# Column and row groups in the q, k, v projection, and the gate logarithms and transposes inside its block

## What is computed

```python
c_qkv, c_beta, c_a = split(hc @ w_in[:, :COL_Z], (COL_BETA, COL_A))     # context tokens
x_qkv, x_beta, x_a, ... = split(hx @ w_in, ...)                         # latent tokens
# gdn_scan, for both
qkv = silu(centred_depthwise_conv(p_qkv, conv_w))        # 5 taps
q, k, v = heads(split(qkv, 3))
q = l2_normalize(q) * HEAD_DIM ** -0.5                   # t * rsqrt(sum(t * t) + EPS)
k = l2_normalize(k)
beta = sigmoid(p_beta)                                   # 2 directions x 8 heads
g = -exp(a_log) * softplus(p_a + dt_bias)
# gated_delta_chunked
G = cumsum(g)                                            # inside a chunk
decay = exp(where(incl, G[..., :, None] - G[..., None, :], -inf))
low = where(strict, (k * beta) @ k.T * decay, 0)
T = inverse(eye + low)                                   # then the scan over the chunks
```

## Time and profile before

| | |
|---|---|
| median of 3 runs | 1741.42 us (1741.04 to 1742.06) |
| profiled execution, first to last instruction | 1744.5 us |
| PE busy | 1535.1 us (88%) |
| DVE, ACT, POOL busy | 811.9, 372.7, 190.5 us |
| mean granted clock of PE | 0.926 of 2.4 GHz |

### The profile page before, as it was taken

The page is one execution under the profiler, slowest core; times in us unless marked ns, Lnnn a source line. Parts: engine busy times, 40 slices in busy tenths (PEclk is TensorE's granted clock), DMA queues, the critical chain, the costliest instruction groups (busy, mean ns, idle before and its releaser), DMA issues. The chain is left out here.

```text
span 1744.5 us, 19526 instructions
## 1 busy us (share of the span) xinstructions
PE 1535.1 (88%) x7573; PEld 898.2 (51%) x7573; DVE 811.9 (47%) x1508; ACT 372.7 (21%) x704; POOL 190.5 (11%) x280
## 2 busy tenths in 40 slices
PE   4999968778999998775889869998989899999977
PEld 2877757478744444342334334443444456656663
DVE  2344548545446567722112123546655225575453
ACT  3122236111111100110001020100540234542230
POOL 0000015700000000011000000000440001213330
PEclk9899979777899999787899989999999899999988
DMA  9331002230497687689999985244220221121120
GB/s 350 106 91 54 0 1 49 82 92 11 129 321 271 232 306 258 276 322 408 410 365 366 390 318 176 97 157 142 64 73 12 85 97 49 49 97 49 50 73 25
DMA packets 132299, 283.62 MB, mean 163 GB/s; under 512 B 28744, under 2 KB 39272, under 8 KB 126955
## 3 DMA queue, kind: packets, MB, share of 16 engines
q1 hardware_dynamic: 128608, 266.65, 42.8%
q0 software_dynamic: 3600, 15.73, 2.2%
HBM read 312.77 MB, written 4.19 MB: 182 GB/s over the span
## 5 line engine op out<-in xcount | busy, mean ns | idle before, releaser
L2717 PE MATMUL ps<-hT,ring 128*128 128x512 f32 x256 | 113.4, 600 | 3.1 <-PEq L2624 2.7
L1402 PE MATMUL ps<-ring,hT 128*128 128x512 f32 x256 | 111.8, 593 | 1.9 <-PEq L184 1.8
L333 DVE SCALAR_TENSOR_TENSOR ada_acc<-ring,cact,ada_acc 128x512 f32<-128x512 f32 x154 | 104.1, 745 | 0.5
L638 PE MATMUL ps<-hT,ring 128*128 128x256 f32 x384 | 90.8, 392 | 5.3 <-PEq L184 5.3
L2352 PE MATMUL ps<-hT,ring 128*128 128x512 f32 x208 | 90.4, 592 | 0.0
L638 PEld LDWEIGHTS ps<-hT,ring 128*128 128x128 f32 x384 | 74.6, 197 | 19.5 <-issue 8.0
L2717 PEld LDWEIGHTS ps<-hT,ring 128*128 128x128 f32 x256 | 48.5, 193 | 61.9 <-issue 61.9
L1402 PEld LDWEIGHTS ps<-ring,hT 128*128 128x128 f32 x256 | 48.0, 190 | 60.3 <-issue 60.0
L1935 PE MATMUL ps<-ring,hT 128*32 128x512 f32 x384 | 54.3, 717 | 25.7 <-DMA ring<-in_expert_w 25.7
L729 DVE SCALAR_TENSOR_TENSOR conv<-xpad,taps,conv 128x512 f32<-128x512 f32 (+1 forms) x96 | 63.6, 663 | 3.4
L2352 PEld LDWEIGHTS ps<-hT,ring 128*128 128x128 f32 x208 | 39.5, 190 | 48.5 <-issue 48.3
(11 more groups left out here) (527 smaller groups left out, 2699.8 us busy)
## 6 DMA issues: line engine op xcount, KB each, us to landing
ring<-in_expert_w SPq DMA_DIRECT2D x24, 2048.0 KB, 15.2
far<-in_expert_w SPq DMA_DIRECT2D x24, 2048.0 KB, 18.3
ring<-in_w_in SPq DMA_DIRECT2D x16, 2048.0 KB, 10.7
ring<-in_ada_w SPq DMA_DIRECT2D x12, 2048.0 KB, 10.4
ring<-in_w_ada SPq DMA_DIRECT2D x12, 2048.0 KB, 9.0
ring<-in_w_in_c SPq DMA_DIRECT2D x10, 2048.0 KB, 7.9
ring<-in_expert_w POOLq DMA_DIRECT2D x32, 512.0 KB
far<-in_expert_w POOLq DMA_DIRECT2D x32, 512.0 KB
```

What stands on the lines that cost most here:

```text
L333: ins = dve.scalar_tensor_tensor(out=part, in0=slot[:, kt], scalar=c[:, kt:kt + 1], in1=part, op0=ALU.mult, op1=ALU.add)
L638: ins = pe.matmul(ps[:, j % BANKS, s * L:(s + 1) * L], slot[:, kt, (j % 4) * P:(j % 4 + 1) * P], (hTc, hTx)[s][:, kt], start=(kt == 0), st ...
L1402: ins = pe.matmul(ps[:, 2 + i % BANKS], hTx[:, kt, t * P:(t + 1) * P], stream.slot(n)[:, kt], start=(kt == 0), stop=(kt == KT - 1))
L2717: ins = pe.matmul(bank, slot[:, kt, j % 4 * P:(j % 4 + 1) * P], hT[:, kt], **edge)
```

## The change

- Beta and gate products: `wba` is stationary (32 columns) and 128 tokens are streamed; the four token tiles go to four quarters of the PSUM partitions. The result has the tokens in the free dimension, so DVE copies it and PE transposes it back before tile 4 (`turn_ba`); DVE splits it (`split_ba`).
- Sums of squares: four calls `sum_squares(b)`, each for four heads with 32 stationary columns into four quarters of bank 7. The squares get eight buffers, which lie in `ktok`.
- Spreads: four calls `spread_norm(b)`, each for four heads from four quarters of the rows into banks 4 to 7.
- The gates' logarithms on ACT move before tiles 9 and 16 (`gates_of_ba`, `logs_of_gates`), their parts on DVE to tiles 12, 15 and 18, the gates' sums on PE before tile 14 (`sum_gates`).
- The transposes follow tile 23 in the same block, k first. ACT copies out the first twelve; of the last four, which wait for silu of the last tile, ACT and DVE copy two each.
- The blocks of the transposes and of the gates' sums are gone. POOL's clears move into the preparation, ahead of the masks of g = 2 and g = 4, and SP waits for them before it loads the first solution.

```diff
...
+N_SQ = 2 * QUADS
+sq = ktok[:, :, :].rearrange("p t d -> p (t d)").rearrange("p (b t) -> p b t", b=N_SQ)
+quad = lambda g: slice(g * WIN, (g + 1) * WIN)
 ssem = stage_sems(scope, "qkv_")
 loaded, proj, padded, conved, silued = ssem("loaded"), ssem("proj"), ssem("padded"), ssem("conved"), ssem("silued")
 pad_zero, taps_t, taps_done = ssem("pad_zero"), ssem("taps_t"), ssem("taps_done")
+GATES_AT, SUM_AT, LOGS_AT = 9, 14, 16
+K_TURNS, V_TURNS = 4 * TT, 2 * TT
+N_TURNS = K_TURNS + 2 * V_TURNS
+def turn_of(i):
+    if i < K_TURNS:
+        return kT, ktok, i // 2, i % 2
+    return vT, vtok, (i - K_TURNS) % V_TURNS, (i - K_TURNS) // V_TURNS
+def move(eng, copy, i):
+    _, dst, t, half = turn_of(i)
+    eng.wait_ge(turned, i + 1)
+    return copy(dst[:, t, half * 512:half * 512 + 512], ps[:, 4 + i % 4])
...
-def sum_squares(j):
+def sum_squares(b):
+    if b == 0:
...
+    pe.wait_ge(squared, QUADS * (b + 1))
+    row = pick_row[:, WIN - 1 - b:2 * WIN - 1 - b]
+    ranges = [(L, 2 * L)] if b < 2 else [(0, L), (L, 2 * L)] if b == 2 else [(0, 2 * L)]
+    for a, e in ranges:
+        for g in range(QUADS):
+            ins = pe.matmul(ps[quad(g), 7, a:e], row, sq[:, (QUADS * b + g) % N_SQ, a:e], start=(b == 0), stop=(b == 3))
+    ins.then_inc(sums, 1)
+def spread_norm(b):
+    a, e = span(QUADS * b)
     pe.wait_ge(inverted, 1)
+    pe.wait_ge(ba_chain, 3)
+    if b:
+        pe.wait_ge(normed, QUADS * b)
+    for g in range(QUADS):
+        ins = pe.matmul(ps[:, 4 + g, a:e], ident[quad(g), g * WIN + b:g * WIN + b + 1].to_broadcast([WIN, P]), norm[quad(g), a:e],
+                        start=True, stop=True)
+    ins.then_inc(spread, 1)
...
+    for kt in range(KT):
+        for t in range(2 * TT):
+            ins = pe.matmul(ps[quad(t), 6, 0:P], wba[:, kt], (hTc, hTx)[t // TT][:, kt, (t % TT) * P:(t % TT + 1) * P],
+                            start=(kt == 0), stop=(kt == KT - 1))
+    ins.then_inc(ba_summed, 1)
+def turn_ba():
+    pe.wait_ge(ba_copied, 1)
+    pe.transpose(ps[:, 6, 0:P], baT[:, :], ident).then_inc(ba_done, 1)
+def sum_gates():
+    pe.wait_ge(ba_chain, 5)
     for t in range(2 * TT):
+        for d in range(2):
+            ins = pe.matmul(ps[:, 6, (2 * t + d) * H:(2 * t + d + 1) * H], tri[:, d], glog[:, t, d * H:(d + 1) * H],
+                            start=True, stop=True)
+    ins.then_inc(g_summed, 1)
+def turn(i):
+    src, _, t, half = turn_of(i)
+    if i == 0:
+        pe.wait_ge(normed, 2 * H)
+    if i >= K_TURNS:
+        pe.wait_ge(silued, 2 * H + 4 * ((i - K_TURNS) // V_TURNS + 1))
+    if i >= 4:
+        pe.wait_ge(moved, i - 3)
+    transpose_in(pe, 4 + i % 4, lambda m: src[:, 4 * half + m, t * P:(t + 1) * P], 4).then_inc(turned, 1)
 for j in range(N_TILES):
+    if j == SUM_AT:
+        sum_gates()
     if j == 2:
         small_products()
+    if j == 4:
+        turn_ba()
...
-        if j >= SPREAD_AT:
-            for m in range(2):
-                spread_norm(2 * (2 * (j - SPREAD_AT) + s) + m)
+        if j >= SPREAD_AT and s == 0:
+            if j == SPREAD_AT:
+                pe.wait_ge(g_copied, 1)
+            spread_norm(j - SPREAD_AT)
...
-    if LAG <= j < 2 * H + LAG:
-        sum_squares(j - LAG)
+    if LAG <= j < 2 * H + LAG and (j - LAG) % QUADS == QUADS - 1:
+        sum_squares((j - LAG) // QUADS)
+for i in range(N_TURNS):
+    turn(i)
...
+def gates_of_ba():
+    act.wait_ge(ba_chain, 3)
+    act.activation(beta[:, :, :], beta[:, :, :], ACT.Sigmoid).then_inc(ba_act, 1)
+    act.activation(sp1[:, 1], sp1[:, 0], ACT.Abs).then_inc(ba_act, 1)
+    act.wait_ge(ba_act, 2)
+    act.activation(sp1[:, 1], sp1[:, 1], ACT.Exp, scale=-1.0)
+    act.activation(rows[:, 0], rows[:, 0], ACT.Exp).then_inc(ba_act, 1)
+    act.wait_ge(ba_act, 3)
+    act.activation(sp1[:, 1], sp1[:, 1], ACT.Ln, bias=1.0).then_inc(ba_act, 1)
+def logs_of_gates():
+    act.wait_ge(g_bounded, 1)
+    act.activation(lnb[:, :, :], lnb[:, :, :], ACT.Ln).then_inc(g_exped, 1)
+    act.wait_ge(g_copied, 1)
+    act.activation(neg[:, :, :], gsum[:, :, :], ACT.Exp).then_inc(g_exped, 1)
+for j in range(N_TILES):
+    if j == GATES_AT:
+        gates_of_ba()
+    if j == LOGS_AT:
+        logs_of_gates()
     if j == 2 * H + LAG:
...
+    pad(j)
...
+for i in range(K_TURNS + V_TURNS):
+    move(act, act.copy, i).then_inc(moved, 1)
+silu(N_TILES - 1)
+for i in range(K_TURNS + V_TURNS, N_TURNS, 2):
+    move(act, act.copy, i)
...
+dve.wait_ge(ba_summed, 1)
+dve.tensor_copy(baT[:, :], ps[:, 6, 0:P]).then_inc(ba_copied, 1)
+def split_ba():
+    dve.wait_ge(ba_done, 1)
+    ba = ps[:, 6, 0:2 * TT * 4 * H].rearrange("p (t c) -> p t c", t=2 * TT)
+    dve.tensor_copy(beta[:, :, :], ba[:, :, 0:2 * H]).then_inc(ba_chain, 1)
+    dve.tensor_tensor(sp1[:, 0], ba[:, :, 2 * H:], rows[:, 1].unsqueeze(1).to_broadcast([P, 2 * TT, 2 * H]),
+                      ALU.add).then_inc(ba_chain, 1)
+    dve.wait_ge(ba_chain, 2)
+    dve.tensor_scalar(sp1[:, 2], sp1[:, 0], 0.0, None, ALU.max).then_inc(ba_chain, 1)
+def decay_logs():
+    dve.wait_ge(ba_act, 4)
+    dve.tensor_scalar(lnb[:, :, :], beta[:, :, :], 1e-37, None, ALU.max).then_inc(g_bounded, 1)
+    dve.tensor_tensor(sp1[:, 2], sp1[:, 2], sp1[:, 1], ALU.add).then_inc(ba_chain, 1)
+    dve.wait_ge(ba_chain, 4)
+    dve.scalar_tensor_tensor(out=glog[:, :, :], in0=sp1[:, 2], scalar=-1.0,
+                             in1=rows[:, 0].unsqueeze(1).to_broadcast([P, 2 * TT, 2 * H]),
+                             op0=ALU.mult, op1=ALU.mult).then_inc(ba_chain, 1)
 def normalize(j):
...
+    dve.wait_ge(spread, j // QUADS + 1)
...
         dve.wait_ge(rooted, 1)
-        dve.reciprocal(inv, inv).then_inc(inverted, 1)
+        dve.reciprocal(norm[:, :], norm[:, :]).then_inc(inverted, 1)
...
+    if j == 4:
+        split_ba()
+    if j == SUM_AT - 2:
+        decay_logs()
+    if j == SUM_AT + 1:
+        dve.wait_ge(g_summed, 1)
+        dve.tensor_copy(gsum[:, :, :], ps[:, 6, 0:4 * TT * H].rearrange("p (t u) -> p t u", t=2 * TT)).then_inc(g_copied, 1)
+    if j == LOGS_AT + 2:
+        dve.wait_ge(g_exped, 2)
+        dve.tensor_scalar(neg[:, :, :], neg[:, :, :], -1.0, None, ALU.mult)
+        dve.tensor_tensor(lnb[:, :, :], lnb[:, :, :], gsum[:, :, :], ALU.subtract)
...
     store_solution(sp, 0)
+    sp.wait_ge(t_zeroed, 2)
     load_solution(sp, 0)
...
+    def clear_solution(b):
+        pool.memset(sols[b], 0.0).then_inc(sol_set[b], 1)
+        pool.wait_ge(sol_set[b], 1)
+        pool.memset(sols[b][:, 0:BLK * BLK:BLK + 1], 1.0).then_inc(sol_set[b], 1)
+        pool.memset(t_of[b][0], 0.0).then_inc(t_zeroed, 1)
     for g in range(2 * PAIRS):
+        if g in (2, 4):
+            clear_solution(g // 2 - 1)
...
```

More of the change, by code:

```diff
@@ L386, in build @@
             vtok = sb(qkv, "vtok", [P, 2 * TT, D])
+            gsum = sb(qkv, "gsum", [P, 2 * TT, 2 * H])
+            neg = sb(qkv, "neg", [P, 2 * TT, 2 * H])
+            lnb = sb(qkv, "lnb", [P, 2 * TT, 2 * H])
             proj_in = qkv.enter_context(ExitStack())
@@ L597, in sum_squares @@
                                 pe.wait_ge(taps_done, 1)
[L598 to L604, removed]
@@ L606, in spread_norm @@
-                        def spread_norm(j):
-                            a, b = span(j)
-                            pe.wait_ge(inverted, 1)
[L609 to L612, removed]
+                            pe.wait_ge(squared, QUADS * (b + 1))
@@ L672, in silu @@
                                 act.wait_ge(silued, j + 1)
[L673 to L677, removed]
+                                if j >= N_SQ:
+                                    act.wait_ge(sums, (j - N_SQ) // QUADS + 1)
+                                act.activation(sq[:, j % N_SQ, a:b], dest(j)[:, 0:L] if j < H else dest(j), ACT.Square).then_inc(squared, 1)
@@ L678, in _ @@
                             if j == 2 * H + LAG:
[L679 to L682, removed]
+                                act.wait_ge(sums, 2 * H // QUADS)
+                                act.activation(norm[:, :], ps[:, 7], ACT.Sqrt, bias=eps[:, 0:1]).then_inc(rooted, 1)
@@ L683, in _ @@
+                            pad(j)
                             if j >= 1:
                                 silu(j - 1)
-                        act.wait_ge(ba_chain, 2)
-                        act.activation(sp1[:, 1], sp1[:, 0], ACT.Abs).then_inc(ba_act, 1)
-                        act.wait_ge(ba_act, 1)
-                        act.activation(sp1[:, 1], sp1[:, 1], ACT.Exp, scale=-1.0)
-                        act.activation(rows[:, 0], rows[:, 0], ACT.Exp).then_inc(ba_act, 1)
-                        act.wait_ge(ba_act, 2)
@@ L692, in _ @@
-                        act.activation(sp1[:, 1], sp1[:, 1], ACT.Ln, bias=1.0).then_inc(ba_act, 1)
+                        for i in range(K_TURNS + V_TURNS):
[3 more added lines that the diff above has]
+                            move(act, act.copy, i)
                     @block.vector
@@ L734, in _ @@
                             ins.then_inc(conved, 1)
```

(2 more changed lines are left out.)

99 lines of the change are left out of this document (10 added, 89 removed).

## The result

The changed kernel takes **1697.81 us** (median of 4 runs, 1695.47 to 1698.68) where the kernel before takes 1741.74 us on the same chip (4 runs, 1741.04 to 1744.65): a ratio of 0.973, 95% interval 0.9706 to 0.9755. The gain is 43.9 us; 40.7 were forecast, and the forecast time was 1701. The profiled execution spans 1697.1 us.

What follows compares the result with a forecast made beforehand. TensorE's instruction stream was taken to bound the projection. Gains of 25.8 us there and 16.6 in the tail, less 1.7 for POOL, made 40.7; from the median 1741.42 that gave 1701 us, range 1692 to 1711.

Steps and rivals of the forecast that it cites:

- Part 1: Before and in the first projection tiles: 32 weight columns stationary, 128 tokens streamed in four column groups; gain 11.4 us.
- Part 2: Between projection tiles: sixteen one-head sums-of-squares calls become four of four heads in overlapping column groups; gain 9.5 us.
- Part 3: In the projection stream: sixteen spread calls become four, each of four heads in overlapping row groups; gain 7.0 us.
- Part 4: Gates' sums move into the projection stream before tile 14, adding 2.1 us there; their old place counts in the tail.
- Part 5: Tail from the last projection product (E) to the preparation's first product: 28.3 becomes 11.7 us, gain 16.6.
- Part 6: In the preparation, POOL's clears stand ahead of two masks and delay its loop; 1.7 us lost, bounds 0 and 3.3.
- estimate of 3 us less: In the projection stream, if a tiling change drains TensorE: change of form costs 0.4 instead of 0.1, gain 3 us smaller.
- What was counted as hidden: Gates' logarithms on ACT and small DVE operations inside the projection cost nothing; without that cover 11 us.
- row groups in turns: Rival on the spreads: row groups do not overlap, the stream loses 2 us instead of gaining 7; 1710 us, chance 0.13.
- the clock falling for good: Rival in projection tiles 6 to 23: inserted calls drop TensorE's clock and it stays low; up to about 1820 us, chance 0.03.
- lost downstream: Rival behind the preparation: a wait for weights swallows the earlier start, no change; about 1741 us, chance 0.02.
- the clock and the tail: Rival: half clock behind beta products and before the last four turns, full clears, dearer weight loads; 1707 us, chance 0.12.

Runs made afterwards that it cites:

- the shared moves: Changed kernel with transposed results copied by ACT alone only for the first seven turns, then by DVE and ACT in turn: 1695.46 us, ratio 0.9718.

## Why the prediction was right, and where its sizes were off

The mechanism held: PE's stream bounded the projection, and what left it left the time. That the sum came so close is in part luck, since errors of either sign offset each other. By terms:

| Step | forecast | measured | from |
|---|---|---|---|
| Part 1, beta and gate products | 11.4 | 11.8 | 10.0 on the products, 1.85 on tiles 2 and 3, turn about 0 |
| Part 2, sums of squares | 9.5 | 11.6 | 16 calls against 4, change of form included, and 0.5 of slot changes beside the old calls |
| Slot changes, not in the sum | 0 | -1.5 | four of 0.50 against one |
| Part 3, spreads in the stream | 7.0 | 7.1 | 11.3 to 4.2, change of form included |
| Part 4, gates' sums | -2.1 | -1.8 | hold 1.70 |
| Projection in all | 25.8 | 27.2 | 0.2 more on the first two tiles, which vary between profiles, makes the 27.5 |
| Part 5, tail | 16.6 | 17.1 | 28.21 to 11.10 |
| Part 6 and the preparation | -1.7 | +1.4 | clears -1.0, clock +2.5 |

**The change of form.** The prediction put it at "some 0.1 a call at most" from the row of L604 alone, and said that this row speaks against the larger price. That step failed. A call in column groups costs 0.30 over its streaming and one in row groups 0.38 in the old kernel, 0.34 and 0.41 for four heads in the new; the rows in front of and behind a call carry the part that the call's own does not. The error made the forecast too small and not too large, because the old stream changed form in 23 calls and the new in 8: 15 calls at about 0.19 not seen in their own rows are 2.9 us for the change. The prediction's estimate of 3 us less had charged the price to the new calls alone; a dearer change of form speaks for fewer calls. Of these 2.9, 2.3 belong to part 2, the most of its surplus; 0.5 more are slot changes. Against this stands that the 12.6 us of the old calls are their busy time, each with a tail that the next product overlaps: from start to start they hold 12.0, so the gain was put 0.6 too high there. The Trainium skill (TensorEngine Tiling (Array Packing), Key Properties) says that a change of tiling mode drains the engine, without a price. The trace agrees in so far as the products on both sides of a call take 0.09 and 0.10 us longer; it does not show what they wait for.

**Slot changes.** Every fourth tile takes a new ring slot. Where two projection products meet there, PE loses 0.50 (the row at 81.02 with its 0.26 idle is the first of four, at tiles 8, 12, 16 and 20); where a sums call stood there, only 0.18 came on top of the call, and `turn_ba` at tile 4 vanishes in it. Before, three of the four had such a call. So the sum lacks 1.5 us, of which 0.5 stood beside the old calls and is in part 2's 11.6; grouping uncovered the other 1.0. What in a slot change costs this, the wait or the release, no run separates.

**Row groups.** That they take turns is refuted: 1.05 for one head, 1.07 for four, each with 512 columns. The four calls hold 3.43 where 3.0 were taken from the calls in column groups; a call in row groups holds more of the change of form. The Trainium skill (TensorE: Matmul & The Clock Gate, Part 3) gives 3.07 times for four row groups, with 512 columns; here sixteen heads hold 13.4 apart and 3.43 together, 3.9 times, and the measurement decides.

**What was counted as hidden** was hidden: there is no gap of PE on ACT's evacuations at tiles 13 or 20 (the 0.26 at tile 20 is the slot change), although ACT's busy time in a stretch of 113 us rose from 25.11 of 112.5 to 37.14.

**The tail** came step by step as worked out: ACT's first move at E + 1.06 (1.05 forecast), its busy row without a gap to E + 7.5, the first late result at E + 8.3 and the last copy at E + 9.6, at full clock. "Late next is ACT" is shown by the shared moves, which take 1.9 us out.

**The preparation** was forecast 1.7 longer and became 1.4 shorter. The clears cost some 1.0 (0.7 to 1.1 return when they move), not 1.7: the argument of g = 3 is made at 220.05, ahead of the product of g = 2 that the first clear delays to 222.03, so part of the delay is made up before the second clear. What was missing is the clock: before, the preparation began at 0.50 (the windows row from 251.30 above), now it begins at 1.00. The prediction put this at nothing, although its own pointed to it, where eight turns behind an idle PE took 6.43. Four cases agree on both terms: where it begins at half clock the preparation takes 37.64 without clears in its loop (before) and 38.75 with them (the gates' block back in); where it begins at full clock, 35.12 without and 35.8 to 36.2 with them.

The rivals: row groups in turns and the clock falling for good did not occur; the shift was not lost downstream (43.8 us up to 700 us). Of "the clock and the tail" one part came once: the clock fell during the beta products in one profile of ten, at 1.6 us. Before the last four turns PE does wait, 1.76 us, but they run at full clock (1.97 us for sixteen products).

## What to carry to other kernels

Price a small call in a dense TensorE stream from the last regular product ahead of it to the second one behind it: its own row shows only part of what a change of form costs, so merging calls gains twice, by overlap and by fewer changes. Interleave products so that neighbours go to different column or row groups. When a pause of TensorE disappears, count the clock of the stage behind it as a term of its own.

## What the runs showed of the hardware that was not expected

- The order of 64 column-group products alone decides between 1.88 and 5.88 us, at a granted clock of 1.00 in both.
- A call of another tiling form costs 0.30 to 0.34 (column groups) or 0.38 to 0.41 us (row groups) beyond its streaming; the calls in the whole array with 8 columns (L663) lengthen only the product behind them, by 0.08.
- The same program may or may not lose the clock: in the middle of the packed beta products it fell to 0.50 for some 3 us in one of ten profiles and stayed at 1.00 in nine. What decides it stays open.
